# Matrix-memory heads: moving the next head's mask, a pair's read-out and the last store in VectorE's queue

## The reference, cut to what matters

```python
dmat = where(causal, b[t] - b[s] + li[s], -inf)        # decay between two tokens
m_t = max(max_s dmat, inter); wts = exp(dmat - m_t)
sc = (q @ k.T) * wts                                   # scores, masked and decayed
hout = (sc @ v) / max(abs(sum_s sc), exp(-m_t))
yc = head_rmsnorm(hout, c_norm) * sigmoid(og) * silu(z)
h = h + yc @ o_w_out
pl = rmsnorm(p @ ple_w, ple_norm); h = h + sigmoid(h @ ple_gate_w) * pl
```

## Time and profile before

| | |
|---|---|
| median of 3 runs | 2289.75 us (2288.11 to 2289.97) |
| profiled execution, its own time | 2295.09 us |
| span in the profile | 2293.3 us |
| mean granted TensorE clock | 0.984 |
| the head loop in the profile | about 790 to 985 us from the span's start |

### The profile page before, as it was taken

How to read it: one execution, slowest core, us unless ns; L and a number is a source line. 1 busy time by engine, 2 the same in 40 slices (tenths; PEclk the granted TensorE clock), 3 DMA queues, 4 the chain that set the end, 5 groups by cost and what they waited for, 6 DMA issues and landing times.

```text
span 2293.3 us, 38564 instructions
## 1 busy us (share of the span) xinstructions
PE 2187.2 (95%) x12244; PEld 1879.9 (82%) x12244; DVE 1226.9 (53%) x1893; ACT 1250.1 (55%) x2249; POOL 1781.3 (78%) x1401
## 2 busy tenths in 40 slices
PE   8999998999999999989998899999999999989997
PEld 6887887888888887878887778888888888867886
DVE  5556765345661267733565754535644664378612
ACT  5475456565545465555664355446655544466654
POOL 6788686988989866789887757776699878645696
PEclk9999999999999999999999999999999999999998
DMA  7565434666667544456665435564476655533464
GB/s 244 179 183 169 124 108 148 187 185 186 186 189 212 178 132 129 125 172 190 184 199 159 147 98 159 174 182 139 136 212 187 198 181 180 176 105 116 133 189 133
DMA packets 211827, 379.05 MB, mean 165 GB/s; under 512 B 23648, under 2 KB 34528, under 8 KB 211552
## 3 DMA queue, kind: packets, MB, share of 16 engines
q1 hardware_dynamic: 207360, 369.52, 53.1%
q10 hardware_dynamic: 4320, 7.66, 1.0%
HBM read 374.99 MB, written 2.10 MB: 164 GB/s over the span
## 4 chain that ended last, share of the span: by engine, by line
PE 39%; POOL 35%; issue 21%; DVE 4%; POOLq 1%; ACT 1%; DVEq 0%; ACTq 0%
POOL w_lo L438 34%; PE ps L517 23%; PE ps L518 12%; PE ps L636 1%; PE ps L785 1%; POOLq L437 1%; DVE ps L1521 0%; DVE tb L1520 0%; DVE w L1526 0%; ACT w_hi L894 0%; PE ps L591 0%; PE ps L547 0%; PE ps L504 0%; PE ps L807 0%; PE ps L505 0%
## 5 line engine op out<-in xcount | busy, mean ns | idle before, releaser
L438 POOL TENSOR_TENSOR w_lo<-raw,w_hi 128x512 fp32r<-128x512 f32 (+1 forms) x1386 | 1766.3, 1295 | 491.3 <-ACT w_hi L894 444.7
L894 ACT ACTIVATE w_hi<-raw 128x512 fp32r<-128x512 f32 (+1 forms) x1420 | 859.2, 619 | 750.2 <-PE ps L518 672.6
L517 PE MATMUL ps<-xa,w_hi 128*128 128x512 f32 x2832 | 1018.8, 403 | 31.2 <-POOL w_lo L438 18.4
L518 PE MATMUL ps<-xa,w_lo 128*128 128x256 f32 x2832 | 796.8, 281 | 0.0
L517 PE MATMUL ps<-xb,w_hi 128*128 128x512 f32 x2160 | 769.0, 401 | 5.8 <-DVE ob L1873 3.0
L517 PEld LDWEIGHTS ps<-xa,w_hi 128*128 128x128 f32 x2832 | 538.2, 190 | 165.2 <-issue 18.9
L518 PE MATMUL ps<-xb,w_lo 128*128 128x256 f32 x2160 | 605.6, 280 | 0.0
L518 PEld LDWEIGHTS ps<-xa,w_lo 128*128 128x128 f32 x2832 | 540.6, 191 | 1.0
L517 PEld LDWEIGHTS ps<-xb,w_hi 128*128 128x128 f32 x2160 | 406.9, 188 | 107.5 <-issue 3.2
L518 PEld LDWEIGHTS ps<-xb,w_lo 128*128 128x128 f32 x2160 | 408.7, 189 | 0.6
L1520 DVE TENSOR_SCALAR tb<-ps 128x512 f32<-128x512 f32 (+1 forms) x120 | 82.4, 687 | 345.7 <-PE ps L518 344.5
(11 more groups left out here) (330 smaller groups left out, 2143.4 us busy)
## 6 DMA issues: line engine op xcount, KB each, us to landing
raw<-w_gate_dram SPq DMA_DIRECT2D x128, 256.0 KB, 3.0
raw<-w_ogz_dram SPq DMA_DIRECT2D x128, 256.0 KB, 3.0
raw<-w_odin_dram SPq DMA_DIRECT2D x128, 256.0 KB, 3.0
raw<-w_evmoba_dram SPq DMA_DIRECT2D x112, 256.0 KB, 3.0
raw<-w_ein_dram SPq DMA_DIRECT2D x96, 256.0 KB, 3.2
raw<-w_evout_dram SPq DMA_DIRECT2D x80, 256.0 KB, 2.9
raw<-w_odgate_dram SPq DMA_DIRECT2D x72, 256.0 KB, 3.0
raw<-w_einz_dram SPq DMA_DIRECT2D x64, 256.0 KB, 3.0
```

Of the source, the lines that this page charges most:

```text
L438: nc.gpsimd.tensor_tensor(w_lo[:, slot, 0:n], raw[:, at, 0:n], w_hi[:, slot, 0:n].bitcast(F32), SUB).then_inc(lo_pool, 1)
L517: mm(ps[:, bank + b, :], w_hi[:, slot, at], x[:, x0 + k, :], start=(k == 0), stop=False)
L518: ins = mm(ps[:, bank + b, 0:T], w_lo[:, slot, at], x[:, x0 + k, 0:T], start=False, stop=(k == st.blocks - 1))
L894: af(w_hi[:, slot, 0:n], raw[:, at, 0:n], ACT.Copy).then_inc(act_rounded, 1)
```

## The change

Only two queues change. In DVE's queue the mask of the next head becomes a function, `masked_gate`, and the norm another, `normalised`. The mask of head hd+1 is issued at the end of head hd: with an even hd ahead of that head's norm, with an odd hd behind it. The store of chunk 3hd moves from ahead of the probabilities to behind them. For head 7 the last ogz pair is stored right behind the variance, and head 7's norm follows it, both ahead of `finish(6)`. In ACT's queue, `keep_ple(7)` moves from behind the second unit of oout's first pair to behind the sixth. Nothing else differs; no work is added or removed.

```diff
                 def ple_norm(p, par, q):
-                    if l == 1 and p == 0 and q in (0, 1):
-                        keep_ple(6 + q)
+                    if l == 1 and p == 0 and q in (0, 5):
+                        keep_ple(6 + q // 5)
...
-            for hd in range(8):
+            def masked_gate(hd):
+
                 dve.wait_ge(ml_s, hd + 1)
                 step.post(tt(sm[:, 0, 0, :], masks[:, M_LSTM, 0, :], ps[:, 5, 0:T], ADD))
                 tt(sm[:, 0, 1, P:T], masks[:, M_LSTM, 1, P:T], ps[:, 5, P:T], ADD).then_inc(ml_mask, 1)
-                gates_chunk(3 * hd)
+
+            def normalised(hd):
+
+                hb = w[:, 16 + 2 * hd:18 + 2 * hd, :]
+                dve.wait_ge(ml_std, hd + 1)
+                inverse(w[:, 41, :], w[:, 42, :], w[:, 43, :])
+                step(tt(hb, hb, along(w[:, 41, :], 2), MUL))
+
+            masked_gate(0)
+            for hd in range(8):
                 dve.wait_ge(ml_e, 4 * hd + 2)
...
                 dve.wait_ge(ml_p, hd + 1)
+                gates_chunk(3 * hd)
                 gates_chunk(3 * hd + 1)
...
+                if hd == 7:
+                    store("ogz", oa, 0, RS_LAYER, 15, 16)
+                    normalised(7)
                 if hd:
                     finish(hd - 1)
                 else:
                     streamed("p1", 0, 0, None, xs, 0)
                 gates_chunk(3 * hd + 2)
-                dve.wait_ge(ml_std, hd + 1)
-                inverse(w[:, 41, :], w[:, 42, :], w[:, 43, :])
-                step(tt(hb, hb, along(w[:, 41, :], 2), MUL))
-            store("ogz", oa, 0, RS_LAYER, 15, 16)
+                if hd < 7 and hd % 2 == 0:
+                    masked_gate(hd + 1)
+                    normalised(hd)
+                elif hd < 7:
+                    normalised(hd)
+                    masked_gate(hd + 1)
             finish(7)
```

## The result

| | before | changed |
|---|---|---|
| median | 2289.75 us (5 runs, 2285.77 to 2291.89) | 2311.85 us (5 runs, 2302.64 to 2315.96) |
| ratio to before | | 1.0092, 95% interval 1.0069 to 1.0114 |
| profiled execution (span) | 2295.09 (2293.3) | 2302.64 (2300.8) |
| the stretch, in the profile | 800.30 to 998.46: 198.16 | 792.13 to 1007.53: 215.40 |

The change makes the kernel 0.9% slower, some 21 us by the ratio (the two medians are 22.1 apart). The forecast was 2303.0, with a range to 2311. The measured time sits at the upper end of it: the median is 0.9 us above 2311, and 1.0092 times the time before is 2310.8.

What follows compares the result with a forecast made beforehand. PE bounds the stage, so DVE's order counts only where PE waits. Terms -3.7 (even heads) + 7.5 (odd) + 3.2 (head 1) + 4.6 (ple1) + 1.6 (clock) = +13.2 us, giving 2303.0 us; range 2291 to 2311.

Steps and rivals of the forecast that it cites:

- even heads: Heads 2, 4, 6: with the store moved, probabilities start 1.22 us earlier off a 2.12 us gap; -3.7 us for three.
- odd heads: Heads 3, 5, 7: norm behind the mask runs into POOL's units, probabilities 2.5 us later each; +7.5 us for three.
- head 1: Head 0's norm behind head 1's mask opens a new PE gap: +2.7 to +3.7 us, taken as +3.2.
- the clock: PE's slow restarts: head 2's 1.64 us loss vanishes, two of four new gaps cost 1.64 each; +1.6 us net.
- clean norm: Rival at heads 1, 3, 5, 7: the norm stays clean; sum -3.6 us, 2286.2 us; chance 0.15.
- gain at the tail: Rival at head 7's end: sigmoids need only the last store; -4.8 in place of +4.6, 2293.6 us; chance 0.10.
- ties lost and clock low everywhere: Rival: every first operation of the norm held and four slow restarts; sum +20.3 us, 2310.1 us; chance 0.10.
- the ties: Norm's first operation beside POOL, heads 1, 3, 5, 7: odd heads +1.99 us if VectorE is first, +3.04 if GpSimd.
- The rival's remark: Argument for the norm staying clean at heads 1, 3, 5, 7: it is clean there today; that case's chance 0.15.
- Head 7 and ple1: finish(6) behind the early last store delays ACT's sigmoids; PE's ple1 gap grows from 6.22 to 10.8 us, +4.6.
- Copy of ple1's pair 7: `keep_ple(7)` three or four units later is hidden, its bank needed a pair later; uncovered, some 0.7 us.

Runs made afterwards that it cites:

- store-only run: Kernel before with only the store of chunk 3hd moved behind the probabilities; 2287.93 us against 2289.80, ratio 0.9987.
- PSUM run: Changed kernel with the norm's variance and factors held in PSUM, same order; 2285.32 us against 2294.70 of before, ratio 0.9960.
- run with the norm ahead: Changed kernel with the norm ahead of the next head's mask in even heads too; 2292.62 us against 2294.70 of before, ratio 0.9997.
- swapped waits: Changed kernel with ScalarE's two waits ahead of the sigmoids in the other order, finish first, then store; 2309.82 us, one run.
- busy-TensorE run: Changed kernel with 11 (head 1) or 15 (heads 3, 5, 7) extra matmuls ahead of the probabilities' wait; 2301.37 us against 2294.22 of before, ratio 1.0035.
- tail-only run: Kernel before with only head 7's end (last store and norm ahead of finish(6)) and ple1's pair 7 copy as changed; 2296.29 us against 2289.80, 1.0027.
- long filling: Changed kernel with 22 (head 1) or 30 (heads 3, 5, 7) extra matmuls ahead of the probabilities' wait; 2311.45 us against 2294.70 of before, ratio 1.0083.
- run with late sigmoids: Kernel before with chunk 3hd's store behind the probabilities and head 7's sigmoids behind ple1's 14th unit, not 4th; 2289.42 us against 2294.22, 0.9979.

## Why the prediction was right

- **Direction and mechanism.** Foretold +13.2 us (0.58%) and slower, measured 0.92% or 21 us. At the even heads, the odd heads, head 1 and ple1 the waits came as described; one term, the clock, was priced far too low. The clean norm (0.15) and the gain at the tail (0.10) did not come; the case "ties lost and clock low everywhere" (2310.1) was nearer in time but only half right: the clock was low everywhere, the ties were not lost.
- **Even heads.** Foretold 0.90 us of wait and -3.7 us; the waits are 0.99, 0.91, 0.91, and the sum -3.6. The moved store was covered, as the store-only run shows.
- **Odd heads and head 1.** Between +1.99 and +3.04 each, I took 2.5. Measured +1.92, +1.83, +1.81: VectorE was first each time, the lower end. Head 1: foretold +2.7 by that end, measured +2.56. By choosing the middle I was 2.6 us too high over the four. The rival's remark that the norm is clean in these places today holds for heads 2, 4 and 6 only: in head 0 of the kernel before L1596 took 1.38 us. It changes no sum. The PSUM run shows the cause itself and the run with the norm ahead shows that the order sets it off.
- **Head 7 and ple1.** Foretold a gap of 10.8 and +4.6; measured 11.07 and +4.6. Both parts of it were tested, the table load (1.3 us) by the swapped waits.
- **Clock.** This is the term that was mis-sized: "two of the four new gaps of 3 to 5 us to cost 1.64 each", +1.6 net. All four gaps, the shortest 2.56 us, were followed by a slow block, and the price was up to 1.9 us for the block and 0.9 for the chunk behind it, where I had priced the block alone. Less head 2's own slow block, which is gone, the clock costs 8.0 us in the stretch: 7.2 in the heads, and 0.8 behind ple1's gap, which I had left out of the sum. The busy-TensorE run agrees for the heads: 8.5 there, less 1.6 for head 2's block, is 6.9. The difference between 13.2 and 17.2 is +6.4 from the clock and -2.6 from the ties, with 0.2 from small ones. That the two errors have opposite signs is luck: with the ties right, the forecast would have been 2300.4 and farther off.
- **Copy of ple1's pair 7.** Put at nothing, and not tried alone. It stands in oout's first pair, so the stretch does not hold it, but the profiles show that it held up nothing: oout's 129th wide product starts 44.45 us behind the first in before, in the tail-only run and in the changed kernel alike.
- **What stays open.** The runs say 21 us (16 to 26), the stretch of one execution 17.2. The changed kernel's profiled execution was the fastest of its five, so more low clock in the others is likely, but only that one execution has a trace. The unchanged code behind the stretch has a spread of its own, too: the 44.45 us from oout's first to its 129th wide product are 45.30 in the profiles with the norm ahead, the norm in PSUM, the long filling and the store only, at a granted clock of 1.00 (989.77 to 1035 with the norm ahead). What sets that is open.

## What to carry to other kernels

Releasing an engine earlier releases whatever is queued behind it as well: here the mask let ScalarE and then GpSimd go, and GpSimd's reads stood in the way of the very operations put behind the mask. Where VectorE must work beside GpSimd, keep one of the two inputs of its operations in PSUM. And price a wait of TensorE by the time to the end of the slow work behind it, not by the wait alone; behind gaps of 2.6 to 3.6 us the slow work cost another 1.5 to 2.8 us each. Before a step is moved ahead, list every semaphore that it and its dependants wait for: the last store was moved ahead of a step that held ScalarE through a second wait.

## What the hardware showed that I had not expected

- VectorE and GpSimd started within 0.01 us of each other at L1595 in heads 1, 3, 5 and 7 (858.53 both in head 3, GpSimd 0.01 us later in the others), and VectorE's operation ran clean each time (0.42 to 0.43 us). I had expected the tie to fall either way.
- A wait of 2.56 us at head 1 was followed by a granted clock of 0.50. Of the waits of 1.6 to 1.8 us in all runs only one, of 1.77 us in the run with late sigmoids, had a slow block behind it (3.65 us). Of the three waits of 2.1 us in before one had the earlier trace rows, and one of three in the tail-only run (a wait of 2.12 us, then 2.72 us from L729 to L734 in place of 1.41).
- Two waits ahead of one activation are not alike: with the wait for finish(6) written second, the table load stood behind it; with the two swapped, it stood behind the store's, and the load was hidden.
